# Query products with weights stationary, and the query root moved into the exponent's scale, in a hybrid attention and convolution block

## The chip, the cores and the metric

The kernel runs on one core of a Trainium2 chip. The metric is the device time of one execution in microseconds, lower is better. Engines: TensorE (PE, with its weight loads as PEld), VectorE (DVE), ScalarE (ACT), GpSimd (POOL) and SyncE (SP), which issues nearly all DMAs.

## What is computed

One layer on 256 tokens of width 1024, all in float32. The reference, cut:

```
h = rmsnorm(x, g_mix)                       # row mean square, then per-channel gain
proj = h @ w_in                             # 1024 x 4608: q, k, v (512 each), u (1024), gates (2048)
q, k, v = 8 heads of 64                     # u = proj[...] + b_glu
o = causal softmax(q k^T * 64 ** -0.5) v    # 256 tokens are one MoBA block: plain causal attention
z = u_a * sigmoid(u_g)                      # then causal depthwise convolution, 31 taps
cz = silu(layernorm(z))
merged = sigmoid(gate_a) * (o @ w_attn_up) + sigmoid(gate_c) * (cz @ w_conv_pw + b_conv_pw)
x = x + merged @ w_out
x = x + square(relu(rmsnorm(x, g_ffn) @ w_ff1)) @ w_ff2
out = rmsnorm(x, g_final)
```

The row root of the first RMSNorm (`rstd`) is a factor per token, so it may be applied behind a product.

## The kernel before

Every float32 product is made of three products in a shorter format: a matrix is split into a high part (ACT's cast, `w_hi`, `a_hi`) and the rest (DVE's subtraction, `w_lo`, `a_lo`), and lo*hi, hi*hi and hi*lo are added up in PSUM.

**Units.** Weights come in units of 4 x 128 rows by 512 columns (1 MB), in four slots. SP loads `raw`, ACT casts it to `w_hi` (`high`), DVE subtracts it to `w_lo` (`low`), both three units ahead of PE. Units 0 to 17 are the nine 512-column blocks of `w_in`, two halves of the 1024 input rows each, in the order `ORDER`: two blocks for the GLU, then queries (block number `Q` = 2, units 4 and 5), keys (units 6 and 7), values (8 and 9), four gate blocks. Units 18 and 19 are the attention's up projection, 20 and 21 the convolution's, 22 to 25 the output projection, and then come the hidden layers in a loop.

**Two forms of product.** `unit` keeps activations stationary: a 128-token piece of `a_lo` or `a_hi` is loaded, and 512 weight columns stream past it. A unit is 2 token tiles x 4 row chunks x 3 products = 24 matmuls, and the result lies tokens by columns. `up`, in the hidden loop, keeps weights stationary: 128 weight columns are loaded, and the 512 columns that stream are the high and the low activations of 256 tokens side by side (`b_both`), followed by 256 columns of high activations past `w_lo`. A unit is 16 such pairs. The result lies columns by tokens; its right half (the cross product with the low activations) has to be added to the left half.

**Program order.** Each engine runs its own list, written as a loop over the unit number n, "step n" below. Between units PE does the attention's work: at step 6 (`S_QT`) it transposes the queries, at step 8 (`S_KT`) the keys, at steps 9 to 12 the scores of the four head pairs, at 10 to 13 the transposes of the probabilities, at 11 to 14 the products with the values, at step 16 (`S_LN`) the transposes of the convolution's result for LayerNorm; inside unit 18 those of `zn`, LayerNorm's result.

ACT's `take(b)` copies block b out of PSUM behind its second unit, with `rstd` as a scale per token, and counts `evac`. For queries and keys the result is `nat`, which PE transposes and `qk_out` copies into `qk_t`. `exps` makes the exponents of a pair of heads in four activations (two of 256 and two of 128 columns) with the bias `nbias` and the constant scale 1/8, and `normalise` multiplies by the inverse sums. In units 2 and 4 (`GLU_AT`) PE transposes the GLU inputs after the first token tile.

DVE's step n is: `row_max` (mask, maxima, `nbias`) for steps 9 to 12, then `low(n + 3)`, the inverse of the sums, and then as many of the 120 convolution steps (128x256 each) as the table `CONV_AT` gives to step n. Step 15 (`S_OLO`) has its five convolutions ahead of `low`, and step 16's LayerNorm needs all of them. At step 18 (`S_SILU`) follow the SiLU, then the gating of the attention's result, which lets ACT copy the bias into PSUM for unit 20 (`set_bias`).

Of the kernel before, what the change touches and what calls it, by code (L numbers as in the profile page):

```python
# [45 lines left out]

S_VEC = 1
GLU_AT = {2: 0, 4: 1}
S_QT, S_KT = 6, 8
S_ATT = 9  # L50
PAIRS = HEADS // 2
S_OLO = S_ATT + 6
# [5 lines left out]
CONV = [(tap, c) for tap in range(1, 10) for c in (0, 1)]  # L58
CONV += [(tap, c) for tap in range(1, 10) for c in (2, 3)]
CONV += [(tap, c) for tap in range(10, TAPS) for c in range(4)]  # L60
CONV_AT = {2: 6, 3: 12, 4: 9, 5: 9, 6: 9, 7: 9, 8: 9, 9: 6, 10: 8, 11: 8, 12: 8, 13: 12, 14: 10, 15: 5}
assert len(CONV) == sum(CONV_AT.values()) == (TAPS - 1) * 4

F32 = mybir.dt.float32
# [24 lines left out]
def build(nc, x, g_mix, w_in, b_glu, w_dw, b_dw, ln_g, ln_b, w_conv_pw, b_conv_pw,  # L89
# [35 lines left out]
    with ExitStack() as ctx:  # L125
        def sb(name, shape, dt=F32):
            return ctx.enter_context(nc.sbuf_tensor(name, shape, dt))

        def sem(name):
            return ctx.enter_context(nc.semaphore(name))  # L130
# [4 lines left out]
        w_lo = sb("w_lo", [P, SLOTS, HK, W], F32R)  # L135


        a_hi = sb("a_hi", [P, KD, T], F32R)
        a_lo = sb("a_lo", [P, KD, T], F32R)
# [27 lines left out]
        stats = sb("stats", [P, TT, 6])  # L167
        mean_var = sb("mean_var", [P, TT, 2])
        ln_var = sb("ln_var", [P, TT])
        smax = sb("smax", [P, PAIRS, 4])  # L170
        nbias = sb("nbias", [P, PAIRS, 4])
        psums = sb("psums", [P, PAIRS, 4])
# [77 lines left out]
        silu_made = sem("silu_made")  # L250
        cz_hi = sem("cz_hi")
        cz_lo = sem("cz_lo")
        qk_tr = sem("qk_tr")
        qk_made = sem("qk_made")
        mask_made = sem("mask_made")
        scored = sem("scored")
        masked = sem("masked")
# [129 lines left out]
        def _(act):  # L387
# [41 lines left out]
            act.wait_ge(fourth_full, 32)  # L429
            nc.scalar.copy(w_hi[:, 3, 0:2], raw[:, 3, 0:2]).then_inc(fourth_hi, 1)  # L430

            def take(b):

                bank = 2 * (b % 2)
                act.wait_ge(used, 2 * b + 2)
                if b == 0:
                    act.wait_ge(rstd_made, 1)
                if b == Q:
                    act.wait_ge(glu_tr, CC)
                if b == GA:  # L440
                    dst, fn = gates[:, 0, :, 0:W], ACT.Copy
                elif b < 2 or b in (Q, K):
# [10 lines left out]
            def qk_out(i, bank):  # L453
                act.wait_ge(qk_tr, i + 1)
                nc.scalar.copy(qk_t[:, i], chunks(bank)).then_inc(qk_made, 1)

            def exps(p):

                act.wait_ge(nbias_made, p + 1)
                for h in range(2):  # L460
                    nc.scalar.activation(probs[:, 256 * h:256 * h + 256], ps[:, SB0 + h, 0:256], ACT.Exp,
                                         bias=nbias[:, p, h:h + 1], scale=SCALE, accum_out=psums[:, p, h:h + 1])
                for h in range(2):
                    last = nc.scalar.activation(probs[:, 512 + 128 * h:640 + 128 * h], ps[:, SB0 + h, 256:384],
                                                ACT.Exp, bias=nbias[:, p, 2 + h:3 + h], scale=SCALE,
                                                accum_out=psums[:, p, 2 + h:3 + h])
                last.then_inc(exp_made, 1)

# [31 lines left out]
            for n in range(U_LOOP):  # L500
# [22 lines left out]
                                             bias=vec[:, V_BDW + c:V_BDW + c + 1]).then_inc(conv_first, 1)  # L523
                if n == U_CONV:
                    set_bias(1)
                if n == S_QT:
                    qk_out(0, TB)
                if n == S_KT:
                    qk_out(1, SB0)
                if n < U_ATTN and n % 2 == 1 and 0 < n // 2 < GA:  # L530
# [10 lines left out]
                if n < U_ATTN and n % 2 == 1 and n // 2 > GA:  # L541
                    take(n // 2)
                if n == S_GATE:
                    act.wait_ge(evac, GA + 1)
# [97 lines left out]
        def _(dve):  # L642
# [85 lines left out]
            for n in range(U_LOOP):  # L728
                if n in GLU_AT:

                    dve.wait_ge(vec_made, 2)
                    for c in (2 * GLU_AT[n], 2 * GLU_AT[n] + 1):
                        dve.wait_ge(glu_sig, c + 1)
                        nc.vector.scalar_tensor_tensor(out=z[:, c, PAD:PAD + T], in0=ps[:, TB + c, 0:T],
                                                       scalar=vec[:, V_BGLU + c:V_BGLU + c + 1], in1=conv[:, c],
                                                       op0=ALU.add, op1=ALU.mult).then_inc(z_made, 1)
                    dve.wait_ge(z_made, 2 * GLU_AT[n] + 2)
                    dve.wait_ge(const_made, 4)
                if S_ATT <= n < S_ATT + PAIRS:
                    row_max(n - S_ATT)  # L740
                if n == S_LN:
# [31 lines left out]
                if n in (U_ATTN, U_ATTN + 1):  # L773

                    col = n - U_ATTN
                    dve.wait_ge(used, n + 1)
                    dve.wait_ge(evac, len(ORDER))
# [152 lines left out]
        def _(pe):  # L930
# [143 lines left out]
            def glu_transposed(hb):  # L1074
                pe.wait_ge(vec_made, 2)
                pe.wait_ge(evac, hb + 1)
                for c in (2 * hb, 2 * hb + 1):
# [3 lines left out]
                            last = transpose(ps[:, TB + c, part * T + t * P:part * T + t * P + P], nat[:, t, col:col + P])  # L1081
                    last.then_inc(glu_tr, 1)

            for n in range(1, U_ATTN):
                b, half = divmod(n, 2)
                if half == 0 and b >= 2:
                    pe.wait_ge(evac, b - 1)
# [4 lines left out]
                if n > 1:  # L1092
# [6 lines left out]
                if n == S_QT:  # L1099
# [3 lines left out]
                if n == S_KT:  # L1103
                    pe.wait_ge(evac, K + 1)
                    transpose_chunks(SB0, lambda t, c: nat[:, t, W + c * P:W + c * P + P]).then_inc(qk_tr, 1)
                if S_ATT <= n < S_ATT + PAIRS:
                    if n == S_ATT:
                        pe.wait_ge(qk_made, 2)
                    else:
                        pe.wait_ge(exp_made, n - S_ATT)  # L1110
                    scores(n - S_ATT)
                if S_ATT + 1 <= n <= S_ATT + PAIRS:
                    probs_transposed(n - S_ATT - 1)
                if S_ATT + 2 <= n < S_ATT + 2 + PAIRS:
                    if n == S_ATT + 2:
                        pe.wait_ge(evac, V + 1)
                    values(n - S_ATT - 2)
                if n == S_LN:

# [22 lines left out]

            for col in range(2):
                pe.wait_ge(o_lo, 1)
                pe.wait_ge(evac, len(ORDER) - 1 + col)
# [102 lines left out]
```

## Time and profile before

| | us |
|---|---|
| median of 3 timed runs | 354.77 (354.44 to 354.78) |
| the profiled execution | 355.19 |
| its span | 353.4 |
| PE busy | 346.9 |
| PE weight loads busy | 287.7 |
| DVE busy | 254.4 |
| ACT busy | 188.7 |

The span begins with the first instruction that the profiler records and ends with the last; the rest of an execution's time lies around it. Matmuls are pipelined, so one matmul's duration overlaps the next one's; what it occupies of PE is the distance between two starts. The same holds, in hundredths, for short operations of DVE and ACT.

### The profile page before, as it was taken

To read this page: it belongs to the slowest core of one execution; us is meant where nothing else is said; L and a number is where in the kernel's file an instruction comes from. 1 tells how busy PE (TensorE), PEld (TensorE's weight loads), DVE (VectorE), ACT (ScalarE), POOL (GpSimd) and SP (SyncE) were. 2 spreads that over 40 slices of the span, in tenths; PEclk is the share of its full clock that TensorE was granted. 3 is DMA by queue.
4 is the path that set the end of the run, shared out by engine and by line. 5 is a ranking of instruction groups with operands and counts; after the bars stand their busy time and mean duration, and the time that the engine had idled before them with its cause. 6 is when DMAs were issued, how large, how long until landed. Compare 5 with 4: busy or idle time off the path is not lost.

```text
span 353.4 us, 4590 instructions
## 1 busy us (share of the span) xinstructions
PE 346.9 (98%) x1729; PEld 287.7 (81%) x1729; DVE 254.4 (72%) x314; ACT 188.7 (53%) x232; POOL 3.5 (1%) x13
## 2 busy tenths in 40 slices
PE   8999999999999999999999999999999999999993
PEld 5888888787778888888888888888888888888883
DVE  2969999999989989956756836638366393663835
ACT  3985654688786358434654535425355153551613
POOL 1000000000000000000000000000000000000000
PEclk9999999999999999999999999999999999999999
DMA  7999455435543364782636471944729547260003
GB/s 269 347 387 378 162 190 185 174 121 153 165 159 119 121 237 165 252 256 106 226 127 239 156 255 66 316 159 153 243 79 304 170 138 249 88 237 0 0 0 120
DMA packets 34431, 64.24 MB, mean 182 GB/s; under 512 B 1361, under 2 KB 6001, under 8 KB 34417
## 3 DMA queue, kind: packets, MB, share of 16 engines
q1 hardware_dynamic: 34112, 63.57, 53.1%
q10 hardware_dynamic: 304, 0.48, 0.4%
q8 instruction: 9, 0.15, 0.2%
q14 instruction: 6, 0.04, 0.0%
HBM read 63.00 MB, written 1.05 MB: 181 GB/s over the span
## 4 chain that ended last, share of the span: by engine, by line
issue 64%; PE 25%; DVE 7%; ACT 2%; POOL 0%; POOLq 0%; DVEq 0%
PE ps L945 6%; PE ps L947 6%; PE ps L946 6%; DVE conv L699 3%; PE ps L932 3%; PE ps L991 2%; DVE w_lo L646 2%; PE ps L1002 1%; PE ps L1045 1%; PE ps L972 1%; DVE res L875 1%; ACT w_hi L396 1%; PE ps L1070 0%; DVE stats L745 0%; ACT gates L450 0%
## 5 line engine op out<-in xcount | busy, mean ns | idle before, releaser
L945 PE MATMUL ps<-w_hi,a_lo 128*128 128x512 f32 x272 | 107.5, 395 | 0.0
L947 PE MATMUL ps<-w_lo,a_hi 128*128 128x512 f32 x272 | 106.1, 390 | 0.0
L946 PE MATMUL ps<-w_hi,a_hi 128*128 128x512 f32 x272 | 106.0, 390 | 0.0
L1175 PE MATMUL ps<-b_both,w_hi 128*128 128x512 f32 x256 | 90.8, 399 | 0.0
L1177 PE MATMUL ps<-b_both,w_lo 128*128 128x256 f32 x256 | 71.9, 281 | 0.0
L860 DVE TENSOR_TENSOR w_lo<-raw,w_hi 128x2048 fp32r<-128x2048 f32 x28 | 63.5, 2288 | 6.4 <-ACT w_hi L600 6.4
L396 ACT CAST w_hi<-raw 128x2048 fp32r<-128x2048 f32 (+1 forms) x30 | 53.7, 1796 | 16.8 <-PE ps L947 16.7
L646 DVE TENSOR_TENSOR w_lo<-raw,w_hi 128x2048 fp32r<-128x2048 f32 x26 | 59.4, 2288 | 3.4 <-ACT w_hi L396 3.3
L945 PEld LDWEIGHTS ps<-w_hi,a_lo 128*128 128x128 f32 x272 | 51.1, 188 | 11.1 <-issue 0.7
L947 PEld LDWEIGHTS ps<-w_lo,a_hi 128*128 128x128 f32 x272 | 51.0, 188 | 11.0
L946 PEld LDWEIGHTS ps<-w_hi,a_hi 128*128 128x128 f32 x272 | 51.1, 188 | 10.0
L1175 PEld LDWEIGHTS ps<-b_both,w_hi 128*128 128x128 f32 x256 | 48.1, 188 | 11.8
L600 ACT CAST w_hi<-raw 128x2048 fp32r<-128x2048 f32 x28 | 52.8, 1912 | 7.8 <-PE ps L947 7.8
L1177 PEld LDWEIGHTS ps<-b_both,w_lo 128*128 128x128 f32 x256 | 48.3, 189 | 0.3
L699 DVE SCALAR_TENSOR_TENSOR conv<-z,dw,conv 128x256 f32<-128x256 f32 x120 | 48.6, 483 | 0.0
L839 DVE TENSOR_TENSOR nat<-ps,nat 128x512 f32<-128x512 f32 x16 | 11.1, 692 | 42.5 <-ACT nat L584 42.5
L584 ACT COPY nat<-ps 128x512 f32<-128x512 f32 x16 | 9.4, 588 | 57.5 <-PE ps L1177 57.5
L590 ACT CAST a_hi<-nat 128x1024 fp32r<-128x1024 f32 x7 | 7.4, 1052 | 21.8 <-PE ps L947 21.6
L852 DVE TENSOR_TENSOR a_lo<-nat,a_hi 128x1024 fp32r<-128x1024 f32 x7 | 8.6, 1223 | 14.1 <-ACT a_hi L590 14.1
L945 PE MATMUL ps<-w_hi,b_both 128*128 128x512 f32 x44 | 17.3, 393 | 0.0
L947 PE MATMUL ps<-w_lo,b_both 128*128 128x512 f32 x44 | 17.1, 389 | 0.0
L946 PE MATMUL ps<-w_hi,b_both 128*128 128x512 f32 x44 | 17.1, 389 | 0.0
(127 smaller groups left out, 259.3 us busy)
## 6 DMA issues: line engine op xcount, KB each, us to landing
raw<-in_w_ff_dram SPq DMA_DIRECT2D x32, 1024.0 KB, 5.4
raw<-in_w_in_dram SPq DMA_DIRECT2D x14, 1024.0 KB, 7.1
raw<-in_w_out_dram SPq DMA_DIRECT2D x4, 1024.0 KB, 5.1
raw<-in_w_in_dram SPq DMA_DIRECT2D x14, 256.0 KB, 5.5
raw<-in_w_attn_up_dram SPq DMA_DIRECT2D x2, 1024.0 KB, 5.0
raw<-in_w_conv_pw_dram SPq DMA_DIRECT2D x2, 1024.0 KB, 4.9
res<-in_x_dram SPq DMA_DIRECT2D x2, 512.0 KB, 4.1
raw<-in_w_in_dram SPq DMA_DIRECT2D x4, 128.0 KB, 4.4
```

Source lines behind the costliest of these rows:

```text
L396: nc.scalar.copy(w_hi[:, n % SLOTS, part], raw[:, n % SLOTS, part]).then_inc(hi_made, 1)
L600: nc.scalar.copy(w_hi[:, slot], raw[:, slot]).then_inc(hi_made, 1)
L646: nc.vector.tensor_tensor(w_lo[:, n % SLOTS], raw[:, n % SLOTS], w_hi[:, n % SLOTS].bitcast(F32), ALU.subtract).then_inc(lo_made, 1)
L699: nc.vector.scalar_tensor_tensor(out=conv[:, c], in0=z[:, c, tap:tap + T], scalar=dw[:, w:w + 1], in1=conv[:, c], op0=ALU.mult, op1=ALU.ad ...
L839: nc.vector.tensor_tensor(hid[:, pair], ps[:, TB + 2 * half:TB + 2 * half + 2, 0:T], hid[:, pair], ALU.add).then_inc(sum_made, 1)
L860: nc.vector.tensor_tensor(w_lo[:, slot], raw[:, slot], w_hi[:, slot].bitcast(F32), ALU.subtract).then_inc(lo_made, 1)
L932: return nc.tensor.transpose(dst, src, ident[0:src.shape[0], 0:src.shape[0]])
L945: nc.tensor.matmul(dst, lo[:, tok], w_hi[:, slot, k], start=start, stop=False, skip_group_check=seeded)
L946: nc.tensor.matmul(dst, hi[:, tok], w_hi[:, slot, k], start=False, stop=False, skip_group_check=seeded)
L947: return nc.tensor.matmul(dst, hi[:, tok], w_lo[:, slot, k], start=False, stop=stop, skip_group_check=seeded)
L1175: nc.tensor.matmul(ps[:, TB + c], w_hi[:, slot, k, cols], b_both[:, kk].rearrange("p a t -> p (a t)"), start=kk == 0, stop=False)
L1177: last = nc.tensor.matmul(ps[:, TB + c, 0:T], w_lo[:, slot, k, cols], b_hi[:, kk], start=False, stop=kk == KD - 1)
```

## The change

Units 4 and 5, the queries, are computed in the second form, with weights stationary. `a_hi` and `a_lo` become the halves of one array `a_both`, as `b_hi` and `b_lo` already are. The result lies columns by tokens, which is how the scores want it: the query transposes and `qk_out(0)` go, and so does `take(2)`. Instead ACT copies the right halves (`queries_cross`, step 5) and DVE adds the left halves (step 6, `S_QADD`). The results lie in the PSUM banks 0, 1, 4 and 5.

The queries are then not multiplied by `rstd`. It is a factor per query token, thus per row of the scores, and goes into the exponent: `q_scale` = `rstd`/8 as a scale per partition in place of the constant, and `q_neg` = -`rstd`/8 in the row maximum's last step. `evac` counts one less from there on, and unit 8 waits for the query adds (`q_made`), since it writes banks 0 and 1.

`CONV_AT` changes at steps 6 to 9 (9, 9, 9, 6 become 7, 8, 8, 5) and 13 (12 becomes 17).

```
-CONV_AT = {2: 6, 3: 12, 4: 9, 5: 9, 6: 9, 7: 9, 8: 9, 9: 6, 10: 8, 11: 8, 12: 8, 13: 12, 14: 10, 15: 5}
+CONV_AT = {2: 6, 3: 12, 4: 9, 5: 9, 6: 7, 7: 8, 8: 8, 9: 5, 10: 8, 11: 8, 12: 8, 13: 17, 14: 10, 15: 5}
...
+            def queries_cross():
+
+                act.wait_ge(used, 2 * Q + 2)
+                for half in range(2):
+                    bank = Q_BANKS[2 * half]
+                    last = nc.scalar.copy(qk_t[:, 0, 2 * half:2 * half + 2], ps[:, bank:bank + 2, T:2 * T])
+                    last.then_inc(q_cross, 1)
...
-                                         bias=nbias[:, p, h:h + 1], scale=SCALE, accum_out=psums[:, p, h:h + 1])
+                                         bias=nbias[:, p, h:h + 1], scale=q_scale[:, 1:2], accum_out=psums[:, p, h:h + 1])
...
-                nc.vector.tensor_scalar(nbias[:, p], smax[:, p], -SCALE, None, ALU.mult).then_inc(nbias_made, 1)
+                nc.vector.tensor_tensor(nbias[:, p], smax[:, p], q_neg[:], ALU.mult).then_inc(nbias_made, 1)
...
+                if n == S_QADD:
+                    for half in range(2):
+                        bank, pair = Q_BANKS[2 * half], slice(2 * half, 2 * half + 2)
+                        dve.wait_ge(q_cross, half + 1)
+                        nc.vector.tensor_tensor(qk_t[:, 0, pair], ps[:, bank:bank + 2, 0:T], qk_t[:, 0, pair],
+                                                ALU.add).then_inc(q_made, 1)
+                    dve.wait_ge(rstd_made, 1)
+                    nc.vector.tensor_scalar(q_scale[:], rstd[:, 0, 0:TT], SCALE, None, ALU.mult).then_inc(q_scaled, 1)
+                    for at, t in ((0, 1), (2, 0)):
+                        nc.vector.tensor_scalar(q_neg[:, at:at + 2], rstd[:, 0, t:t + 1].to_broadcast([P, 2]), -SCALE, None,
+                                                ALU.mult).then_inc(q_scaled, 1)
...
+            def queries(n):
+
+                weights(n)
+                for c in range(CC):
+                    if n == 2 * Q and c == 2:
+                        pe.wait_ge(z_made, 2)
+                    cols = slice(c * P, c * P + P)
+                    for k in range(HK):
+                        kk = HK * (n % 2) + k
+                        nc.tensor.matmul(ps[:, Q_BANKS[c]], w_hi[:, n % SLOTS, k, cols],
+                                         a_both[:, kk].rearrange("p a t -> p (a t)"), start=kk == 0, stop=False)
+                        last = nc.tensor.matmul(ps[:, Q_BANKS[c], 0:T], w_lo[:, n % SLOTS, k, cols], a_hi[:, kk],
+                                                start=False, stop=kk == KD - 1)
+                    if n == 2 * Q and c == 1:
+                        glu_transposed(GLU_AT[n])
+                last.then_inc(used, 1)
...
+                if n == 2 * V:
+                    pe.wait_ge(q_made, 2)
...
-                if n == S_QT:
-                    pe.wait_ge(evac, Q + 1)
+                if n == S_KT:
+                    pe.wait_ge(evac, K)
                     pe.wait_ge(z_made, CC)
-                    transpose_chunks(TB, lambda t, c: nat[:, t, c * P:c * P + P]).then_inc(qk_tr, 1)
```

On PE, at the end of unit 6 (keys, first half), the kernel before has the query transposes between two products:

```order
L946 MATMUL ps<-w_hi,a_hi 128x512
L947 MATMUL ps<-w_lo,a_hi 128x512
L932 MATMUL ps<-ident,nat 128x128 x8
L945 MATMUL ps<-w_hi,a_lo 128x512
```

In the changed kernel, at the end of unit 5 (queries, second half; L1120 and L1122 are the two products of `queries`) and the start of unit 6:

```order
L1120 MATMUL ps<-a_both,w_hi 128x512
L1122 MATMUL ps<-a_both,w_lo 128x256
L972 MATMUL ps<-w_hi,a_both 128x512
L973 MATMUL ps<-w_hi,a_both 128x512
L974 MATMUL ps<-w_lo,a_both 128x512
```

The eight transposes are gone from PE's list, and units 4 and 5 consist of such pairs.

On DVE, steps 5 to 9, before (L646 is `low`, L699 a convolution step, L707 the mask of the first row maximum):

```order
L699 SCALAR_TENSOR_TENSOR conv<-z,dw,conv 128x256 x9
L646 TENSOR_TENSOR w_lo<-raw,w_hi 128x2048
L699 SCALAR_TENSOR_TENSOR conv<-z,dw,conv 128x256 x9
L646 TENSOR_TENSOR w_lo<-raw,w_hi 128x2048
L699 SCALAR_TENSOR_TENSOR conv<-z,dw,conv 128x256 x9
L646 TENSOR_TENSOR w_lo<-raw,w_hi 128x2048
L699 SCALAR_TENSOR_TENSOR conv<-z,dw,conv 128x256 x9
L707 TENSOR_TENSOR ps<-ps,mask 128x2x256
```

and in the changed kernel (L660, L713 and L721 are the same three):

```order
L713 SCALAR_TENSOR_TENSOR conv<-z,dw,conv 128x256 x9
L757 TENSOR_TENSOR qk_t<-ps,qk_t 128x512 x2
L760 TENSOR_SCALAR q_scale<-rstd 128x2
L762 TENSOR_SCALAR q_neg<-rstd 128x2 x2
L660 TENSOR_TENSOR w_lo<-raw,w_hi 128x2048
L713 SCALAR_TENSOR_TENSOR conv<-z,dw,conv 128x256 x7
L660 TENSOR_TENSOR w_lo<-raw,w_hi 128x2048
L713 SCALAR_TENSOR_TENSOR conv<-z,dw,conv 128x256 x8
L660 TENSOR_TENSOR w_lo<-raw,w_hi 128x2048
L713 SCALAR_TENSOR_TENSOR conv<-z,dw,conv 128x256 x8
L721 TENSOR_TENSOR ps<-ps,mask 128x2x256
```

Two adds and three small multiplications came in ahead of step 6's `low`, and four convolution steps left.

On DVE, steps 12 to 15, up to the first work of LayerNorm (L719 is the inverse of the last pair's sums), before:

```order
L719 RECIPROCAL rinv<-psums 128x4
L699 SCALAR_TENSOR_TENSOR conv<-z,dw,conv 128x256 x8
L646 TENSOR_TENSOR w_lo<-raw,w_hi 128x2048
L699 SCALAR_TENSOR_TENSOR conv<-z,dw,conv 128x256 x12
L646 TENSOR_TENSOR w_lo<-raw,w_hi 128x2048
L699 SCALAR_TENSOR_TENSOR conv<-z,dw,conv 128x256 x15
L646 TENSOR_TENSOR w_lo<-raw,w_hi 128x2048
```

and in the changed kernel:

```order
L733 RECIPROCAL rinv<-psums 128x4
L713 SCALAR_TENSOR_TENSOR conv<-z,dw,conv 128x256 x8
L660 TENSOR_TENSOR w_lo<-raw,w_hi 128x2048
L713 SCALAR_TENSOR_TENSOR conv<-z,dw,conv 128x256 x17
L660 TENSOR_TENSOR w_lo<-raw,w_hi 128x2048
L713 SCALAR_TENSOR_TENSOR conv<-z,dw,conv 128x256 x15
L660 TENSOR_TENSOR w_lo<-raw,w_hi 128x2048
```

Five convolution steps came in between the `low` of unit 16 and that of unit 17.

## Rows read from the trace of the kernel before

**Rows 1.** The page's busy line: busy us, share of the span, instructions.
```profile
PE 346.9 (98%) x1729; PEld 287.7 (81%) x1729; DVE 254.4 (72%) x314; ACT 188.7 (53%) x232; POOL 3.5 (1%) x13
```

**Rows 2.** The waits of PE: who waited for whom, total, times, longest us.
```profile
PE ps L972 <- DVE zero_b L649: 1.2, 1, 1.2
```

**Rows 3.** The chain of waits in order of time, ahead of step 13: start, us, what.
```profile
96.61 1.80 ACT w_hi L396
98.44 2.29 DVE w_lo L646
```

**Rows 4.** Timeline of PE, unit 6 and the query transposes: start us, us, engine, line.
```profile
43.01 0.39 PE L945 MATMUL ps<-w_hi,a_lo 128*128 128x512 f32 x1
...
48.46 1.03 PE L932 MATMUL ps<-ident,nat 128*128 128x128 f32 x8
...
49.56 0.40 PE L946 MATMUL ps<-w_hi,a_hi 128*128 128x512 f32 x1
```

**Rows 5.** Timeline of PE, two units of `up` (32 pairs) in the hidden loop.
```profile
203.46 0.39 PE L1175 MATMUL ps<-b_both,w_hi 128*128 128x512 f32 x1
...
214.75 0.40 PE L945 MATMUL ps<-w_hi,a_lo 128*128 128x512 f32 x1
```

**Rows 6.** Groups: DVE's add, ACT's 128x256 from PSUM: busy us, mean ns | idle.
```profile
L839 DVE TENSOR_TENSOR nat<-ps,nat 128x512 f32<-128x512 f32 x16 | 11.1, 692 | 42.5 <-ACT nat L584 42.5
...
L461 ACT ACTIVATE probs<-ps,nbias 128x256 f32<-128x256 f32 x8 | 3.8, 481 | 0.8 <-DVE nbias L715 0.8
...
L553 ACT ACTIVATE conv<-ps,vec 128x256 f32<-128x256 f32 x4 | 1.9, 564 | 0.5 <-PE ps L932 0.5
...
L515 ACT ACTIVATE conv<-ps,vec 128x256 f32<-128x256 f32 x4 | 1.7, 494 | 2.0 <-PE ps L932 2.0
...
L484 ACT COPY o_t<-ps 128x256 f32<-128x256 f32 x4 | 1.5, 374 | 3.6 <-PE ps L1070 3.6
```

**Rows 7.** Timeline of DVE: step 6's start, and two small operations.
```profile
50.60 2.30 DVE L646 TENSOR_TENSOR w_lo<-raw,w_hi 128x2048 fp32r<-128x2048 f32 x1
...
118.21 0.25 DVE L748 BATCH_NORM_AGGREGATE mean_var<-stats 128x2 f32<-128x6 f32 x2
```

**Rows 8.** Timeline of all engines, exponents and normalising of pair 0.
```profile
69.90 0.48 ACT L461 ACTIVATE probs<-ps,nbias 128x256 f32<-128x256 f32 x1 [0.57 <-DVE nbias L715]
...
71.41 0.21 ACT L464 ACTIVATION_READ_ACCUMULATOR probs<-ps,nbias 128x1 f32 x1
71.97 0.17 DVE L719 RECIPROCAL rinv<-psums 128x4 f32<-128x4 f32 x1
...
72.99 0.68 ACT L478 ACTIVATE probs<-probs,rinv 128x128 f32<-128x128 f32 x2
...
74.04 0.64 PEld L932 LDWEIGHTS ps<-ident,probs 128*128 128x128 f32 x6
```

**Rows 9.** Timeline of DVE, steps 13 to 15, and LayerNorm's transposes on PEld.
```profile
100.65 4.84 DVE L699 SCALAR_TENSOR_TENSOR conv<-z,dw,conv 128x256 f32<-128x256 f32 x12
105.40 2.29 DVE L646 TENSOR_TENSOR w_lo<-raw,w_hi 128x2048 fp32r<-128x2048 f32 x1
107.60 6.03 DVE L699 SCALAR_TENSOR_TENSOR conv<-z,dw,conv 128x256 f32<-128x256 f32 x15
113.54 2.29 DVE L646 TENSOR_TENSOR w_lo<-raw,w_hi 128x2048 fp32r<-128x2048 f32 x1
...
115.38 1.02 PEld L932 LDWEIGHTS ps<-ident,conv 128*128 128x128 f32 x8
```

**Rows 10.** Timeline of DVE and ACT from step 16 to the bias, and PEld's load for unit 20.
```profile
120.92 4.49 DVE L646 TENSOR_TENSOR w_lo<-raw,w_hi 128x2048 fp32r<-128x2048 f32 x2
126.88 0.99 DVE L762 TENSOR_SCALAR zn<-ps,vec 128x256 f32<-128x256 f32 x2 [1.47 <-ACT conv L553]
...
132.30 1.13 ACT L498 COPY ps<-gfin_bc 128x512 f32<-128x512 f32 x2 [1.42 <-DVE nat L780]
...
133.50 0.19 PEld L945 LDWEIGHTS ps<-w_hi,b_both 128*128 128x128 f32 x1
```

More of the change, by code:

```diff
@@ L48 @@
 GLU_AT = {2: 0, 4: 1}
-S_QT, S_KT = 6, 8
+Q_BANKS = (0, 1, 4, 5)
+S_QADD, S_KT = 6, 8
 S_ATT = 9
@@ L135, in build @@
         w_lo = sb("w_lo", [P, SLOTS, HK, W], F32R)
-        a_hi = sb("a_hi", [P, KD, T], F32R)
-        a_lo = sb("a_lo", [P, KD, T], F32R)
+        a_both = sb("a_both", [P, KD, 2, T], F32R)
+        a_hi, a_lo = a_both[:, :, 0], a_both[:, :, 1]
         b_both = sb("b_both", [P, KD, 2, T], F32R)
@@ L169, in build @@
         ln_var = sb("ln_var", [P, TT])
+        q_scale = sb("q_scale", [P, TT])
+        q_neg = sb("q_neg", [P, 4])
         smax = sb("smax", [P, PAIRS, 4])
@@ L252, in build @@
         cz_lo = sem("cz_lo")
-        qk_tr = sem("qk_tr")
-        qk_made = sem("qk_made")
+        q_cross = sem("q_cross")
+        q_made = sem("q_made")
+        q_scaled = sem("q_scaled")
+        k_tr = sem("k_tr")
+        k_made = sem("k_made")
         mask_made = sem("mask_made")
@@ L437, in take @@
                     act.wait_ge(rstd_made, 1)
-                if b == Q:
+                if b == K:
                     act.wait_ge(glu_tr, CC)
@@ L441, in take @@
                     dst, fn = gates[:, 0, :, 0:W], ACT.Copy
-                elif b < 2 or b in (Q, K):
+                elif b < 2 or b == K:
                     dst, fn = nat[:, :, (b % 2) * W:(b % 2) * W + W], ACT.Copy
@@ L451, in take, with keys_out @@
                 last.then_inc(evac, 1)
-            def qk_out(i, bank):
-                act.wait_ge(qk_tr, i + 1)
-                nc.scalar.copy(qk_t[:, i], chunks(bank)).then_inc(qk_made, 1)
+            def keys_out():
+                act.wait_ge(k_tr, 1)
+                nc.scalar.copy(qk_t[:, 1], chunks(SB0)).then_inc(k_made, 1)
             def exps(p):
@@ L461, in exps @@
                     nc.scalar.activation(probs[:, 256 * h:256 * h + 256], ps[:, SB0 + h, 0:256], ACT.Exp,
-                                         bias=nbias[:, p, h:h + 1], scale=SCALE, accum_out=psums[:, p, h:h + 1])
+                                         bias=nbias[:, p, h:h + 1], scale=q_scale[:, 1:2], accum_out=psums[:, p, h:h + 1])
                 for h in range(2):
                     last = nc.scalar.activation(probs[:, 512 + 128 * h:640 + 128 * h], ps[:, SB0 + h, 256:384],
-                                                ACT.Exp, bias=nbias[:, p, 2 + h:3 + h], scale=SCALE,
+                                                ACT.Exp, bias=nbias[:, p, 2 + h:3 + h], scale=q_scale[:, 0:1],
                                                 accum_out=psums[:, p, 2 + h:3 + h])
@@ L525, in _ @@
                     set_bias(1)
-                if n == S_QT:
-                    qk_out(0, TB)
                 if n == S_KT:
-                    qk_out(1, SB0)
-                if n < U_ATTN and n % 2 == 1 and 0 < n // 2 < GA:
+                    keys_out()
+                if n == 2 * Q + 1:
+                    queries_cross()
+                elif n < U_ATTN and n % 2 == 1 and 0 < n // 2 < GA:
                     take(n // 2)
@@ L543, in _ @@
                 if n == S_GATE:
-                    act.wait_ge(evac, GA + 1)
+                    act.wait_ge(evac, GA)
                     part = gates[:, 0, :, 0:W]
@@ L738, in _ @@
                     dve.wait_ge(const_made, 4)
+                if n == S_QADD:
[9 more added lines that the diff above has]
+                                                ALU.mult).then_inc(q_scaled, 1)
+                if n == S_ATT:
+                    dve.wait_ge(q_scaled, 3)
                 if S_ATT <= n < S_ATT + PAIRS:
@@ L776, in _ @@
                     dve.wait_ge(used, n + 1)
-                    dve.wait_ge(evac, len(ORDER))
+                    dve.wait_ge(evac, len(ORDER) - 1)
                     dve.wait_ge(gate_made, 1)
@@ L1086, in _ @@
                 if half == 0 and b >= 2:
-                    pe.wait_ge(evac, b - 1)
+                    pe.wait_ge(evac, b - 1 if b <= V - 1 else b - 2)
+                if n == 2 * V:
+                    pe.wait_ge(q_made, 2)
                 if n == 2:
@@ L1091, in _ @@
                     pe.wait_ge(fourth_lo, 1)
-                if n > 1:
+                if b == Q:
+                    queries(n)
+                elif n > 1:
                     unit(n, a_hi, a_lo, HK * half, lambda t: 2 * (b % 2) + t, half == 0, half == 1,
@@ L1098, in _ @@
                     transpose(ps[:, SB0 + 1, P:P + TAPS * CC], dw_rows).then_inc(vec_tr, 1)
[L1099 to L1100 removed]
+                if n == S_KT:
+                    pe.wait_ge(evac, K)
                     pe.wait_ge(z_made, CC)
[L1102 to L1105 removed]
+                    transpose_chunks(SB0, lambda t, c: nat[:, t, W + c * P:W + c * P + P]).then_inc(k_tr, 1)
                 if S_ATT <= n < S_ATT + PAIRS:
                     if n == S_ATT:
[L1108 removed]
+                        pe.wait_ge(k_made, 1)
+                        pe.wait_ge(q_made, 2)
                     else:
@@ L1115, in _ @@
                     if n == S_ATT + 2:
-                        pe.wait_ge(evac, V + 1)
+                        pe.wait_ge(evac, V)
                     values(n - S_ATT - 2)
@@ L1144, in _ @@
                 pe.wait_ge(o_lo, 1)
-                pe.wait_ge(evac, len(ORDER) - 1 + col)
+                pe.wait_ge(evac, len(ORDER) - 2 + col)
                 unit(U_ATTN + col, b_hi, b_lo, 0, lambda t: 2 * (1 - col) + t, True, True,
```

## The prediction

> **What bounds the kernel now.** The page's busy line comes first: TensorE (PE) is busy 346.9 of 353.4 us [rows 1]. The waits view, asked for PE alone, has one line, 1.2 us at the start [rows 2]. So PE's queue is the bound, and a change is worth what it takes from that queue, as long as no other engine comes late to it. Who could? The chain of waits in order of time answers: between the scores and LayerNorm it goes over ScalarE's weight cast into VectorE's (DVE's) queue [rows 3]. PE does not stop for that chain, but the chain has the least slack here. I therefore work out PE's own work first, and then the places at which DVE or ScalarE (ACT) must be done before PE goes on: the conv deadline and the bias deadline below.
>
> **PE's own work.** Units 4 and 5 are the query products. Unit 6 has the old form, 24 matmuls of 512 columns: it starts at 43.01, the next thing on PE at 48.46, so 5.45 us [rows 4]. The new form is that of `up` in the hidden loop: two units, 32 pairs of a 512 and a 256 column matmul, run from 203.46 to 214.75, 11.29 us [rows 5]. Two old units take 10.90, so the new form costs +0.39 to +0.41 (starts are rounded to hundredths; I take 0.41). The columns streamed are equal (48 x 512 against 32 x 768); the difference comes with 64 weight loads instead of 48. The eight query transposes go. They push the second product of the next unit from 48.69 (43.01 and 25 starts of 0.227) to 49.56 [rows 4]: -0.87. PE reaches unit 6's end, and all that follows, 0.46 us earlier. The GLU transposes inside unit 4 stay.
>
> By the Trainium skill (page TensorE: Matmul & The Clock Gate, "Back-to-back issue gap") a warm matmul takes N/2.4 + 2.5 ns: 216 for 512, 109 for 256. A pair would be 0.325 us and two new units 0.02 us dearer than two old ones, not 0.41. The trace disagrees (0.353 for a pair, 0.227 for 512 columns). The sum would be the same by either, since PE would only wait longer at the second deadline below; only where the gain is carried (a rival) would it count.
>
> **DVE before attention.** Step 6 gets two adds of 128x512 out of PSUM and three tiny multiplications. Such an add takes 0.69 [rows 6]. An instruction of DVE overlaps the next by some 0.09: two tiny ones of 0.17 [rows 8] take 0.25 together [rows 7]. So an add holds the queue 0.60, a tiny one 0.08. That is 1.20 + 0.25 = +1.45 us. Four convolution steps leave steps 6 to 8 (9, 9, 9 become 7, 8, 8); twelve run from 100.65 to 105.40, 0.396 each [rows 9], so -1.58. The first row maximum, which follows its predecessor in DVE's queue, comes 0.1 us earlier. Unit 8 now waits for the adds: they start behind step 5's convolutions, at 50.60 [rows 7], and end by 52.0; unit 8 starts at 54.3. Covered by over 2 us. ACT's two copies of the crossed half replace `take(2)`, and its `qk_out(0)` goes; ACT waits for PE there, so this is worth nothing.
>
> **The exponents.** Their scale becomes a per-partition operand beside the bias. The trace has no such exponent. Activations of 128x256 out of PSUM take 374 ns without such an operand, 481 (these exponents) and 494 (a sigmoid) with one, 564 with two [rows 6]. So an operand costs 70 to 107 ns; from 481 to 564 is 83. Four exponents a head pair: +0.33 us (0.28 to 0.43) on ACT's chain.
>
> **First deadline: the probabilities of pair 0.** The exponents started at 69.90 and their last read ended at 71.62 [rows 8]; now 69.80 and 71.85. DVE's reciprocal started at 71.97 behind a weight subtraction, now 71.87: the exponents are just in time. Normalising ended at 73.67, now 73.57. PE's first transpose of them loaded at 74.04 [rows 8], now wants to at 73.58. With a hand-over of a few hundredths PE loses about 0.05: it is 0.41 early.
>
> **Second: LayerNorm's transposes.** This is the step that decides. The exponents of pair 3 start behind PE's scores and values, thus 0.41 earlier, but end 0.33 later relative to that: -0.08. ACT's cast for unit 16 ends so much earlier, and DVE's subtraction that waits for it moves from 98.44 [rows 3] to 98.36. Step 13 now has 17 convolutions, not 12: +1.98. The last convolution ended at 113.63, with the subtraction behind it at 113.54 [rows 9]. The new order, added up from 98.36: 2.21 to the convolutions, 17 x 0.396, 2.20 for the next subtraction (105.40 to 107.60), 5.94 for the fifteen of steps 14 and 15, gives 115.44 for that subtraction and 115.53 for the result. PE loaded the first transpose of the convolution at 115.38 [rows 9] and would now be ready at 114.97. It waits about 0.6 us and goes on near 115.56. The gain of 0.41 is gone, and PE stands at +0.18 (a wait of 0.59). The 1.75 us of slack that the old order had here (115.38 less 113.63) is what hid DVE's work; five convolutions behind the ACT-gated subtraction use more than all of it.
>
> **Third: the bias for unit 20.** DVE's queue from here is +1.90. Its two subtractions end at 125.41, now 127.31; the SiLU step started at 126.88 after idling and now starts about 127.23, +0.35. It feeds, DVE and ACT alternating, the bias copies that end at 133.43, while PE loads unit 20's first weights at 133.50 [rows 10]: slack 0.07. The bias is +0.35, PE was +0.18, so PE stands at +0.30 afterwards. Behind that DVE is again fed by PE, so 0.30 is carried through the loop, whose work is the same.
>
> **Sum.** -0.87 + 0.41 + 0.05 + 0.59 + 0.12 = +0.30 us. The profiled execution, 355.19 (span 353.4), becomes 355.5. The three timed runs have a median of 354.77, 0.42 lower, and I give the forecast on that: 355.1. About 0.2% (0.7 us) is what a measurement can tell from no change.
>
> **Rivals.**
> - *The gain is carried.* If the deadlines don't bind, PE keeps its -0.46: 354.3. For it: PE stops nowhere today, and the waits are inferred within hundredths. Against it: even with exponents at their old cost the conv deadline moves by 1.98 less 0.46, to 115.15, against 114.92 for PE; that case alone gives about 354.6. In part is thus likelier than whole. By the Trainium skill's gap rule (TensorE: Matmul & The Clock Gate) this case would end 0.4 lower, at 353.9; I give that 3 in 100, since no row shows such a pair.
> - *Slower, by the first deadline.* It has no slack left, and from there every tenth of ACT or DVE comes through all three deadlines. If the five don't overlap (0.69 and 0.17 each instead of 0.60 and 0.08: +0.44) and each exponent pays 107 ns (+0.10), normalising ends 0.54 later, PE waits 0.6 there, and the exponents' extra tenth comes once more before the conv deadline: +0.30 + 0.54 + 0.1, 355.7. It decides when DVE's and ACT's additions before pair 0 exceed 0.4 us above mine.
> - *No saving on PE at all*: if the query products' loads cost more than in the hidden loop, by the 0.87 that the transposes give back, PE has +0.41 in place of -0.46 before attention, the exponents of pair 3 and all behind them come 0.82 later than above, and the end is 1.1 later than now: 355.9. The same instructions in the loop speak against it.
>
> **How the numbers follow.** Forecast (both late deadlines bind, +0.1 to +0.5): 0.62. Gain kept in part or whole (-0.46 to 0.1): 0.20, of which 0.03 lie beyond 0.2%. Slower by one of the two mechanisms: 0.18, some two thirds of it beyond 0.2%. Range: 354.3, the gain whole, to 355.8, the slower cases with a tenth for the spread of the runs; 1 to 2 in 10 lie outside. Faster by over 0.2%: 0.05; within: 0.82; slower: 0.13.
>
> **What would show it.** In the trace of the changed kernel: the query products take 11.3 us less the GLU transposes, and unit 6 starts 0.4 later, unit 7 0.46 earlier. The exponents of 128x256 take some 0.565 us. DVE's run of 17 convolutions ends near 107.3, the last before LayerNorm near 115.5. PE idles 0.5 to 0.6 us ahead of the transposes of `conv`, released by DVE; unit 20 starts 0.1 late. If PE does not idle at `conv`, the second deadline is wrong and the time is near 354.3. If it idles over 0.3 at the first transposes of `probs`, the slower rival holds. If pairs take other than 0.353 us, the first term is wrong.

## The result and the profile after

The changed kernel takes 355.25 us (median of 22 runs, 354.65 to 355.8), the kernel before 354.74 (22 runs beside them). The ratio is 1.0012 with a 95% interval of [1.0006, 1.0017]: 0.43 us slower, 0.2 to 0.6 (the medians alone differ by 0.51). The forecast was +0.30, and 355.1 us.

The page of the changed kernel, its busy line (columns as in [rows 1]):

```profile
PE 346.0 (98%) x1737; PEld 286.9 (81%) x1737; DVE 256.0 (72%) x319; ACT 189.2 (54%) x231; POOL 3.5 (1%) x13
```

PE is busy 0.9 us less. PE's waits had only the line of the start [rows 2]. They and the new ones of its weight loads (PEld) now read:

```profile
PE ps L999 <- DVE zero_b L663: 1.2, 1, 1.2
PE ps L959 <- ACT probs L492: 0.5, 1, 0.5
PE ps L959 <- DVE conv L713: 0.2, 1, 0.2
...
PEld ps L959 <- ACT probs L492: 0.7, 1, 0.7
PEld ps L959 <- DVE conv L713: 0.7, 1, 0.7
...
PEld ps L972 <- ACT ps L512: 0.3, 1, 0.3
```

These are the three places of the forecast: the transposes of the probabilities (L959 <- L492, ACT's normalising), those of the convolution (L959 <- L713, DVE), and unit 20's first load (L972 <- L512, the bias copies). A matmul's modelled end hides part of PE's own waits, so I go by those of PEld. They say where PE is held; how much of it is lost is measured below by marks, since PE makes up part of such a wait afterwards.

PE's own work, from the timeline of PE (start us, us, engine, line), answering [rows 4, 5]:

```profile
30.48 0.39 PE L1120 MATMUL ps<-a_both,w_hi 128*128 128x512 f32 x1
...
33.30 1.03 PE L959 MATMUL ps<-ident,nat 128*128 128x128 f32 x8
...
34.52 0.40 PE L1120 MATMUL ps<-a_both,w_hi 128*128 128x512 f32 x1
...
42.50 0.39 PE L972 MATMUL ps<-w_hi,a_both 128*128 128x512 f32 x1
```

Units 4 and 5 with the GLU transposes between go from 30.48 to 42.50, 12.02 us. The first eight pairs take 0.353 each (30.48 to 33.30), the last 23 take 0.347 (34.52 to 42.50); between them lie the transposes and one pair.

The queries on DVE, from its timeline, answering [rows 7]:

```profile
50.29 1.29 DVE L757 TENSOR_TENSOR qk_t<-ps,qk_t 128x512 f32<-128x512 f32 x2
51.49 0.17 DVE L760 TENSOR_SCALAR q_scale<-rstd 128x2 f32<-128x2 f32 x1
51.55 0.24 DVE L762 TENSOR_SCALAR q_neg<-rstd 128x2 f32<-128x2 f32 x2
51.69 2.29 DVE L660 TENSOR_TENSOR w_lo<-raw,w_hi 128x2048 fp32r<-128x2048 f32 x1
```

The five additions hold DVE's queue from 50.29 to 51.69, 1.40 us.

Exponents and normalising of pair 0, timelines of ACT, DVE and PEld, answering [rows 8]:

```profile
69.40 0.56 ACT L475 ACTIVATE probs<-ps,nbias,q_scale 128x256 f32<-128x256 f32 x1 [1.44 <-DVE nbias L729]
...
71.27 0.21 ACT L478 ACTIVATION_READ_ACCUMULATOR probs<-ps,nbias,q_scale 128x1 f32 x1
...
72.54 0.68 ACT L492 ACTIVATE probs<-probs,rinv 128x128 f32<-128x128 f32 x2
```
```profile
71.51 0.18 DVE L733 RECIPROCAL rinv<-psums 128x4 f32<-128x4 f32 x1
```
```profile
73.27 0.64 PEld L959 LDWEIGHTS ps<-ident,probs 128*128 128x128 f32 x6 [0.71 <-ACT probs L492]
```

The four exponents with their reads take 2.08 us (69.40 to 71.48), 0.36 more than before (69.90 to 71.62). Normalising ends at 73.22 (72.54 + 0.68), and PE loads 0.05 later, after its weight loads have idled for 0.71.

Steps 13 to 15 and LayerNorm's transposes, timelines of DVE and PEld, answering [rows 9]:

```profile
100.22 6.82 DVE L713 SCALAR_TENSOR_TENSOR conv<-z,dw,conv 128x256 f32<-128x256 f32 x17
106.95 2.29 DVE L660 TENSOR_TENSOR w_lo<-raw,w_hi 128x2048 fp32r<-128x2048 f32 x1
109.15 6.03 DVE L713 SCALAR_TENSOR_TENSOR conv<-z,dw,conv 128x256 f32<-128x256 f32 x15
```
```profile
115.23 0.86 PEld L959 LDWEIGHTS ps<-ident,conv 128*128 128x128 f32 x8 [0.66 <-DVE conv L713]
```

The last convolution ends at 115.18 (109.15 + 6.03), and PE's weight loads idle 0.66 us for it. The bias, answering [rows 10]:

```profile
133.48 0.19 PEld L972 LDWEIGHTS ps<-w_hi,b_both 128*128 128x128 f32 x1 [0.31 <-ACT ps L512]
```

**One scale for all kernels.** Two executions differ by up to 0.8 us in when PE gets going: its first GLU transposes, in unit 2 and untouched by the change, start at 22.19 before and at 21.44 after. I therefore count PE's marks from that point in each kernel. Four marks: the loads for the scores of pair 1, for the transposes of pair 0's probabilities, for those of the convolution, and for unit 20. For the kernel before they stand at 51.00, 51.85, 93.19 and 111.31. The last matmul of the program starts at 325.58 on this scale. What each kernel has more or less at a mark (us), and its timed difference (ratio less 1, times 354.8):

| kernel | scores 1 | probs 0 | conv | unit 20 | last matmul | timed |
|---|---|---|---|---|---|---|
| changed | -0.62 | -0.02 | +0.60 | +0.73 | +0.64 | +0.43 |
| e1_old_conv | +0.33 | +1.21 | +1.21 | +1.21 | +1.21 | +1.17 |
| e2_before_new_conv | -0.01 | 0.00 | +0.28 | +0.40 | +0.32 | +0.21 |
| e3_const_scale | -0.62 | -0.48 | -0.20 | -0.07 | -0.16 | -0.07 |
| e4_transposes_back | +0.28 | +0.28 | +0.91 | +1.02 | +0.97 | +1.10 |
| e5_conv_12 | -0.62 | -0.44 | -0.42 | -0.42 | -0.42 | -0.07 |
| e6_conv_8_9 | -0.61 | -0.61 | +0.02 | +0.14 | +0.09 | -0.04 |
| e7_both | -0.62 | -0.62 | -0.62 | -0.62 | -0.61 | -0.64 |
| e8_both_transposes | +0.27 | +0.28 | +0.28 | +0.28 | +0.28 | +0.25 |
| e9_before_both | -0.01 | 0.00 | 0.00 | 0.00 | 0.00 | -0.14 |

A step between two of the four marks is how late a held load is that the kernel before does not hold. The changed kernel: 0.62 gained, 0.60 lost at the probabilities, 0.62 at the convolution, 0.13 at the bias.

The held load is not what PE loses in the end. Behind the transposes of the convolution the next unit's first load stands at 94.18 in the kernel before and at 94.62 in the changed one, from lines of PEld before and after:

```profile
116.37 0.19 PEld L945 LDWEIGHTS ps<-w_hi,a_lo 128*128 128x128 f32 x1
```
```profile
116.06 0.19 PEld L972 LDWEIGHTS ps<-w_hi,a_both 128*128 128x128 f32 x1
```

So PE is +0.44 there, not +0.60. Where PE does not wait, a matmul starts 0.23 after its load (115.38 and 115.61 before); a load that PE is held for has used up that lead, and the eight transposes take 0.86 on PEld instead of 1.02. The column of the last matmul has this in it. Net, the changed kernel loses 0.60 at the probabilities, 0.46 at the convolution and 0.20 at the bias and behind it, and ends at +0.64 in this one execution.

### The profile page after: what moved, and what is told of

It is laid out like the page before. It is cut to its first block, busy times and chain, and to the rows that moved or that the text cites. A ratio compares the mean times of both kernels' runs of the same rounds, so it can differ in the third digit from the quotient of the medians.

```text
span 353.3 us, 4612 instructions
## 1 busy us (share of the span) xinstructions
PE 346.0 (98%) x1737; PEld 286.9 (81%) x1737; DVE 256.0 (72%) x319; ACT 189.2 (54%) x231; POOL 3.5 (1%) x13
## 4 chain that ended last, share of the span: by engine, by line
issue 65%; DVE 21%; PE 5%; ACT 5%; DMA 2%; SPq 2%; POOL 0%; POOLq 0%; DVEq 0%; ACTq 0%
DVE conv L713 10%; DVE w_lo L660 7%; DMA raw<-in_w_in_dram 2%; ACT w_hi L402 2%; SPq L321 1%; PE ps L972 1%; PE ps L974 1%; PE ps L973 1%; PE ps L959 1%; DVE res L902 1%; PE ps L1072 0%; DVE z L748 0%; PE ps L1097 0%; POOL rstd L385 0%; DVE w_lo L668 0%
## 5 line engine op out<-in xcount | busy, mean ns | idle before, releaser
L972 PE MATMUL ps<-w_hi,a_both 128*128 128x512 f32 x256 | 101.2, 395 | 0.0
L974 PE MATMUL ps<-w_lo,a_both 128*128 128x512 f32 x256 | 100.0, 391 | 0.0
L973 PE MATMUL ps<-w_hi,a_both 128*128 128x512 f32 x256 | 99.9, 390 | 0.0
L660 DVE TENSOR_TENSOR w_lo<-raw,w_hi 128x2048 fp32r<-128x2048 f32 x26 | 59.4, 2287 | 3.1 <-ACT w_hi L402 3.0
L972 PEld LDWEIGHTS ps<-w_hi,a_both 128*128 128x128 f32 x256 | 48.1, 188 | 10.5 <-issue 0.7
L974 PEld LDWEIGHTS ps<-w_lo,a_both 128*128 128x128 f32 x256 | 48.1, 188 | 10.3
L973 PEld LDWEIGHTS ps<-w_hi,a_both 128*128 128x128 f32 x256 | 48.1, 188 | 9.5
L713 DVE SCALAR_TENSOR_TENSOR conv<-z,dw,conv 128x256 f32<-128x256 f32 x120 | 48.5, 482 | 0.0
L604 ACT CAST a_both<-nat 128x1024 fp32r<-128x1024 f32 x7 | 7.4, 1053 | 21.8 <-PE ps L974 21.6
L879 DVE TENSOR_TENSOR a_both<-nat,a_both 128x1024 fp32r<-128x1024 f32 x7 | 8.6, 1226 | 14.1 <-ACT a_both L604 14.1
L972 PE MATMUL ps<-w_hi,b_both 128*128 128x512 f32 x44 | 17.4, 396 | 0.0
```

The source lines that it names most:

```text
L660: nc.vector.tensor_tensor(w_lo[:, n % SLOTS], raw[:, n % SLOTS], w_hi[:, n % SLOTS].bitcast(F32), ALU.subtract).then_inc(lo_made, 1)
L713: nc.vector.scalar_tensor_tensor(out=conv[:, c], in0=z[:, c, tap:tap + T], scalar=dw[:, w:w + 1], in1=conv[:, c], op0=ALU.mult, op1=ALU.ad ...
L972: nc.tensor.matmul(dst, lo[:, tok], w_hi[:, slot, k], start=start, stop=False, skip_group_check=seeded)
L973: nc.tensor.matmul(dst, hi[:, tok], w_hi[:, slot, k], start=False, stop=False, skip_group_check=seeded)
L974: return nc.tensor.matmul(dst, hi[:, tok], w_lo[:, slot, k], start=False, stop=stop, skip_group_check=seeded)
```

## The experiments

My theory was the forecast's: PE's gain is real and is taken back by three late arrivals of DVE and ACT. The rival was that the 0.4 us are work that the change adds to an engine, with the convolution table of no weight; a second rival, tested with the first run, was that the waits swallow whatever PE saves.

**The transposes back.** In the changed kernel, at step 6 on PE:

```
+                if n == S_QADD:
+                    pe.wait_ge(z_made, CC)
+                    transpose_chunks(SB0, lambda t, c: res[:, t, c * P:c * P + P])
```

> The changed kernel with eight transposes put back on PE at step 6 (of the input, into a free bank, used by nobody). PE's list then has the removed 0.87 us again, and nothing else moves. Deadline theory: only the wait at the first transposes of the probabilities can swallow PE's work; the wait at the convolution's transposes (0.6 us) is measured from PE's own scores of pair 3 and stays. In the medians the first wait is worth about 0.3 us (0.43 = -0.61 + first wait + 0.62 + 0.13), so the time rises by 0.87 - 0.3 = 0.6 us over the changed kernel: 355.8. Rival, all of the saving is swallowed behind DVE whatever PE does: 355.25. Rival, no wait swallows anything: 356.1.

Measured: 355.78 us, ratio to before 1.0031 [1.0021, 1.0041]. That is 0.53 above the changed kernel by the medians, 0.67 by the ratios, where 0.6 was expected. So only the first wait swallows work of PE (in the trace 0.60 of the 0.90, down to none), and the other two are still there in full:

```profile
PEld ps L959 <- DVE conv L713: 0.7, 1, 0.7
PEld ps L972 <- ACT ps L512: 0.3, 1, 0.3
```

The second rival falls, and with it a wrong picture that the forecast's wording invites: the wait at the convolution does not measure PE's lead. DVE's step 13 starts behind ACT, and ACT behind PE's own scores, so whatever PE gains ahead of the scores moves that deadline too.

**Step 13's surplus to step 12.** In the changed kernel:

```
-... 12: 8, 13: 17, ...
+... 12: 11, 13: 14, ...
```

> The changed kernel with three convolution steps moved from step 13 (17 to 14) to step 12 (8 to 11), where DVE idles 1.36 us for ACT's cast. Deadline theory: the convolutions end 1.19 us earlier, PE no longer waits at the convolution's transposes (0.62) nor for the bias (0.13): 355.25 - 0.75 = 354.5. Rival, the 0.4 us come from work added to PE or ACT: 355.25, unchanged.

Measured: 354.81 us, ratio 0.9998 [0.9989, 1.0007]. 0.44 below the changed kernel by the medians, 0.50 by the ratios, where 0.75 was expected. In the trace the two late waits are gone (-0.44, -0.42, -0.42 in the table) and one is left, the first:

```profile
PEld ps L959 <- ACT probs L492: 0.3, 1, 0.3
```

The expected 0.75 took the two waits by their held loads; net they are 0.66 (0.46 and 0.20). The expected 354.5 would be a ratio of 0.9991, at the edge of the interval. The profiled execution, 354.0, is the fastest of the eleven. The rival "added work", which wanted 355.25, falls.

**And step 8's to step 9.**

```
-... 8: 8, 9: 5, ... 12: 8, 13: 17, ...
+... 8: 6, 9: 7, ... 12: 11, 13: 14, ...
```

> As the one before, and two convolution steps moved from step 8 (8 to 6) to step 9 (5 to 7), behind the first row maximum. Deadline theory: the first row maximum and with it the probabilities of pair 0 come 0.79 us earlier, the first wait (about 0.3) goes as well, PE keeps what it saved (0.6): 354.2, faster than both kernels. Rival, work added: 355.25.

Measured: 354.30 us, ratio 0.9982 [0.9973, 0.9990], 0.64 us faster than before and 0.95 below the changed kernel by the medians. PE waits for nothing but the start:

```profile
PE ps L999 <- DVE zero_b L663: 1.2, 1, 1.2
```

and DVE fills the idle time ahead of ACT's cast, of which 1.36 in the changed kernel became 0.17 us (the end of step 12 and step 13 in DVE's timeline):

```profile
93.10 4.42 DVE L713 SCALAR_TENSOR_TENSOR conv<-z,dw,conv 128x256 f32<-128x256 f32 x11
97.68 2.29 DVE L660 TENSOR_TENSOR w_lo<-raw,w_hi 128x2048 fp32r<-128x2048 f32 x1 [0.17 <-ACT w_hi L402]
99.89 5.63 DVE L713 SCALAR_TENSOR_TENSOR conv<-z,dw,conv 128x256 f32<-128x256 f32 x14
```

This version beats both kernels, with the same instructions as the changed one in another order on DVE.

**Both moves and the transposes back.** The two edits above together.

> The kernel with both moves, with the eight unused transposes put back. Deadline theory: no wait is left to swallow work of PE, so all 0.87 us show: 355.05, 0.87 above the kernel with both moves. Rival, waits still swallow part: less than 0.5 above it.

Measured: 354.98 us, ratio 1.0007 [0.9998, 1.0016]. That is 0.68 above `e7_both` by the medians, 0.89 by the ratios, and 0.90 in the trace (table). With the waits gone, PE's work counts in full. It also prices the removed part by itself: 0.90 us for eight transposes in the trace, against the 0.87 of the forecast.

**The old table in the changed kernel.**

```
-CONV_AT = {... 6: 7, 7: 8, 8: 8, 9: 5, ... 13: 17, ...}
+CONV_AT = {... 6: 9, 7: 9, 8: 9, 9: 6, ... 13: 12, ...}
```

> The changed kernel with the old table of convolution steps. Deadline theory: four more convolution steps lie ahead of the first row maximum (+1.58 us), so the first wait grows from about 0.3 to 1.9 us, while the wait at the convolution's transposes and the one for the bias go (5 x 0.396 = 1.98 less in step 13): -0.61 + 1.9 = +1.3 against the kernel before, 356.0. Rival, the table is of no weight: 355.25. Rival, the late deadline alone counts and the first one does not bind: 354.2.

Measured: 355.96 us, ratio 1.0033 [1.0022, 1.0044]. The first wait grows to 1.83 us in all, since PE is now held twice, at the scores of pair 1 and at the transposes of pair 0's probabilities (timeline of PEld); of the idle time ahead of the scores, 0.35 is there in every kernel:

```profile
72.79 0.73 PEld L1072 LDWEIGHTS ps<-qk_t 64*128 64x128 f32 x8 [1.29 <-ACT probs L478]
74.52 0.53 PEld L959 LDWEIGHTS ps<-ident,probs 128*128 128x128 f32 x5 [1.00 <-ACT probs L492]
```

(The 1.00 holds 0.12 that lie between the two loads in the kernel before too.) After that nothing is lost: +1.21 at every later mark. The change needed a new table: with the old one it is 1.2 us slower than before. The new table paid for pair 0 with the convolution's deadline, where it overdrew.

**The new table in the kernel before.** The same edit the other way round, in the kernel before:

```
-CONV_AT = {... 6: 9, 7: 9, 8: 9, 9: 6, ... 13: 12, ...}
+CONV_AT = {... 6: 7, 7: 8, 8: 8, 9: 5, ... 13: 17, ...}
```

> The kernel before with the new table of convolution steps alone. Deadline theory: the convolutions end 1.98 us later, 0.23 beyond the 1.75 of slack, so PE waits 0.3 at the convolution's transposes; DVE's later queue shifts the SiLU by about 0.4, the bias wait adds 0.1: +0.4, 355.15. Rival, the table is of no weight: 354.75.

Measured: 355.01 us, ratio 1.0006 [0.9997, 1.0015]. By the timed runs alone this is not clear of nothing; the trace shows the two waits at 0.28 and 0.12, where 0.3 and 0.1 were expected, and +0.32 at the last matmul:

```profile
PEld ps L945 <- ACT ps L498: 0.3, 1, 0.3
PEld ps L932 <- DVE conv L699: 0.3, 1, 0.3
```

**The exponents' scale a constant again.**

```
-                                         bias=nbias[:, p, h:h + 1], scale=q_scale[:, 1:2], accum_out=psums[:, p, h:h + 1])
+                                         bias=nbias[:, p, h:h + 1], scale=SCALE, accum_out=psums[:, p, h:h + 1])
...
-                                                ACT.Exp, bias=nbias[:, p, 2 + h:3 + h], scale=q_scale[:, 0:1],
+                                                ACT.Exp, bias=nbias[:, p, 2 + h:3 + h], scale=SCALE,
```

> The changed kernel with the exponents' scale as the constant 1/8 again (the rows' root is then left out of the exponent, so the attention's result is another one). It measures the second operand's cost by itself: exponents of 128x256 fall from 0.56 to 0.48 us, four of them and their reads from 2.08 to 1.72. Deadline theory: the reciprocal of pair 0 still stands behind a weight subtraction, so the first wait stays; from pair 3 on everything is 0.36 earlier: 355.25 - 0.36 = 354.9. Rival, the operand is hidden: 355.25.

Measured: 354.84 us, ratio 0.9998 [0.9989, 1.0007], 0.41 below the changed kernel by the medians. The exponents are back at 0.48:

```profile
69.45 0.48 ACT L475 ACTIVATE probs<-ps,nbias 128x256 f32<-128x256 f32 x1 [1.02 <-DVE nbias L729]
...
70.96 0.21 ACT L478 ACTIVATION_READ_ACCUMULATOR probs<-ps,nbias 128x1 f32 x1
```

1.72 us for the four against 2.08. The waits at the convolution and at the bias are 0.28 and 0.13: the operand's 0.36 came back once, in the convolution's deadline (0.62 to 0.28, 0.34). The first wait was 0.14 here, and the operand has no part in that one: normalising starts 0.21 behind the start of DVE's reciprocal in both kernels (71.53 and 71.74 here, 71.51 and 71.72 in the changed one), and the exponents are done before it in both. `e5_conv_12`, with the dearer exponents, has a first wait of 0.18.

**Only step 8's to step 9.** In the changed kernel, with step 13 left at 17:

```
-... 8: 8, 9: 5, ...
+... 8: 6, 9: 7, ...
```

> The changed kernel with only the move of two convolution steps from step 8 to step 9. Deadline theory: the first wait (0.3 in the medians) goes, the two late ones stay, 354.95. Rival, the first deadline does not bind: 355.25.

Measured: 354.81 us, ratio 0.9999 [0.9990, 1.0008]: 0.44 below the changed kernel where 0.30 was expected. The first wait is gone (-0.61 at both marks), the late two stay (+0.63, +0.12), and the last matmul stands at +0.09.

**The moves in the kernel before.**

```
-CONV_AT = {... 8: 9, 9: 6, ... 12: 8, 13: 12, ...}
+CONV_AT = {... 8: 7, 9: 8, ... 12: 11, 13: 9, ...}
```

> The kernel before with the same kind of moves: two convolution steps from step 8 to step 9, three from step 13 to step 12. Deadline theory: the kernel before waits nowhere, so its time stays, 354.75 to 354.85. Rival, the moves are worth something by themselves: below 354.5.

Measured: 354.86 us beside 354.75, ratio 0.9996 [0.9987, 1.0006]. The marks are those of the kernel before. The moves are worth nothing where PE waits for nothing; `e7_both` is fast by PE's saved work.

## Why the prediction was right, and where it was off

The direction, the size (+0.30 against +0.43 with an interval from 0.2 to 0.6) and the three places hold. That the two sums lie so close is in part luck, since four terms were off and cancel. Term by term:

- Query products: +0.41 forecast. The trace gives 12.02 us for units 4 and 5 with the GLU transposes; the same stretch of the kernel before, 12 starts of 0.227 ahead of its transposes at 33.97 to the 43.01 of [rows 4], is 11.77. So +0.25. The pair at 0.353 [rows 5] held for the first eight and then fell to 0.347. The Trainium skill (page TensorE: Matmul & The Clock Gate, "Back-to-back issue gap") gives N/2.4 + 2.5 ns for an isolated matmul and says that this is too much for a stream of wide ones. By it a pair would take 0.325 at most, an estimate from that figure, and this trace has more, 0.353 and 0.347. (Two new units would by it be 0.04 dearer than two old ones, not 0.02: 16 more matmuls at 2.5 ns.)
- Transposes: -0.87 forecast, -0.87 found (-0.62 at the scores less the +0.25 above), and 0.90 when `e8_both_transposes` puts them back.
- DVE's additions in step 6: 1.45 forecast, 1.40 found. Exponents: +0.33 forecast, +0.36 found, and `e3_const_scale` shows where it comes back.
- Convolution: a wait of 0.59 forecast. The load is held 0.62, but 0.46 of it is lost: the forecast left out that PE makes some of it up in the transposes behind. Bias: 0.12 forecast, the load held 0.13, 0.20 lost by the last matmul.
- **First wait: 0.05 forecast, 0.60 in the profiled execution, some 0.38 in the timed runs** (0.43 = -0.61 + x + 0.46 + 0.20, an estimate that leaves 0.15 to 0.55 by the interval, and takes the start of an execution to be the same in both kernels). This is the term that was mis-sized most. With it, +0.33, the saving of 0.61 for 0.46 (-0.15), the convolution (-0.13) and the bias (+0.08) make +0.43 out of +0.30.

In the first wait the hand-over was right: PE loads 0.05 us after normalising ends. What failed is the place of DVE relative to PE. I took it from one execution. In the changed kernel DVE is busy without a gap from the GLU's products (25.40) to the row maximum, so it does not follow PE there; their distance is what the start of the execution left. What sets it there was not traced.

From PE's first GLU transposes to the start of the first row maximum the changed kernel has 45.97 us (21.44 to 67.41), `e3_const_scale` 45.54 (21.91 to 67.45), `e5_conv_12` 45.56 (21.37 to 66.93), `e4_transposes_back` 46.12 (21.50 to 67.62), with the same DVE list up to there.

The two row maxima, from DVE's timeline of the changed kernel and of `e5_conv_12`:

```profile
67.41 0.70 DVE L721 TENSOR_TENSOR ps<-ps,mask 128x512 f32<-128x512 f32 x1
```
```profile
66.93 0.69 DVE L721 TENSOR_TENSOR ps<-ps,mask 128x512 f32<-128x512 f32 x1
```

That spread of 0.6 us goes straight into the first wait: 0.60 in the changed kernel, 0.18 in `e5_conv_12`, 0.14 in `e3_const_scale`. The forecast's own 0.1 earlier than the 45.70 of the kernel before (22.19 to 67.89) is what two of the four executions have. All eight traces of the changed kernel and its variants, with two or four convolution steps of 0.396 added or taken off where the table differs, and for `e8_both_transposes` the 0.73 that DVE idles just before, give 45.54 to 46.12 and a mean of 45.74. From that start PE's load follows 5.86 later (67.41 to 73.27), and without a wait it would stand at 51.23 (51.85 less 0.62). That makes a mean wait of 0.37, an estimate that agrees with the 0.38 of the timed runs. The kernel before hides it with slack, 0.37 us at this transpose. PE's larger gain (0.62, not 0.46) adds 0.16 to the same wait, since PE arrives earlier and the data do not. So the too high price for the query products and the too low one for the wait cancel in part. Which execution a profile shows decides between 0.1 and 0.6 us of wait here, so the +0.64 of the changed kernel's trace is not its average.

Of the rivals, "the gain is carried" was never on as the kernel stood, but is what the two moves in `e7_both` make of it: -0.64, the whole gain. "Slower by the first deadline" named the right mechanism and had the point right, that there is no slack left; it took the threat to be dearer operations, where it was the spread between two engines' starts. `e1_old_conv` shows it in the large: 1.83 us of wait. The forecast's sign for this rival, over 0.3 us of idling at the first transposes of `probs`, was there (0.71 idle, 0.60 lost), and yet the time is 355.25 and not 355.7: the sign did not tell the two apart, because the dearer operations were not there (1.40 us of additions on DVE where 1.45 was forecast).

## What to carry to other kernels

When an edit takes work off the bound engine and adds it elsewhere, follow both engines to the next point where they meet, and count the slack there: here 0.37 us of reserve at one transpose and 1.75 at another decided over 0.62 us of saved work. A filler such as the convolution steps belongs where its engine idles for somebody else (1.36 us ahead of ACT's cast), not behind that idle time. A deadline that hangs on the bound engine's own earlier work moves with it and does not swallow a gain (the load at the convolution is held 0.62 or 0.63 in the changed kernel, in `e4_transposes_back` and in `e6_conv_8_9`, though PE stands at -0.02, +0.28 and -0.61 before it); one that hangs on an engine that runs freely does.

## What the runs showed that was not expected

- A wait of PE at short transposes costs less than the held load says: 0.62 held and 0.46 lost at the convolution, 0.28 and 0.11 in `e2_before_new_conv`.
- The pairs of a 512 and a 256 column matmul take 0.353 us in the hidden loop and in the first eight query pairs, but 0.347 behind the GLU transposes (`e7_both` alike: six pairs from 31.08 to 33.20, then 22 from 34.78 to 42.41). In the hidden layers, transposes stand between pairs too, and 0.353 holds behind them (58 pairs from 171.68 on, in the kernel before). What sets the difference was not tried and stays open.
- Two engines' starts drift by 0.6 us between executions (45.54 to 46.12 above), while PE's own marks agree within 0.02 us where it does not wait (-0.61 and -0.62, +0.27 and +0.28 in the table). Counting from a mark that the change does not touch made 0.1 us readable in single traces, where the timed runs need a dozen executions for 0.3.
